# A two-block transformer kernel: the latents' compressed rows move from VectorE to ScalarE, VectorE's row work in 11 pieces

## The reference

```
c_kv, k_rope, k_g, v_g = split(kvc)          # 256, 32, 128, 128 columns
kv    = rms_norm(c_kv, g_ckv) @ w_ukv
k_gqa = apply_rope(rms_norm(k_g per head, g_kn_gqa))
c_q, q_g = split(qc)                         # 384, 512 columns
q_mla = rms_norm(c_q, g_cq) @ w_uq
q_gqa = apply_rope(rms_norm(q_g per head, g_qn_gqa))
y = sigmoid(gates) * branches
```

## Time and profile before

| | us |
|---|---|
| median of three executions | 2631.74 |
| the profiled execution | 2632.22 |
| its span | 2630.4 |
| TensorE matmuls busy | 2502.9 (95%) |
| VectorE busy | 1617.4 (61%) |
| ScalarE busy | 1325.9 (50%) |
| GpSimd busy | 585.1 (22%) |

### The profile page before, as it was taken

How to read it: one execution, slowest core, us unless ns; L and a number is a source line. 1 busy time by engine, 2 the same in 40 slices (tenths; PEclk the granted TensorE clock), 3 DMA queues, 4 the chain that set the end, 5 groups by cost and what they waited for, 6 DMA issues and landing times. The chain is left out here.

```text
span 2630.4 us, 46361 instructions
## 1 busy us (share of the span) xinstructions
PE 2502.9 (95%) x17358; PEld 2210.2 (84%) x17358; DVE 1617.4 (61%) x2415; ACT 1325.9 (50%) x2127; POOL 585.1 (22%) x429
## 2 busy tenths in 40 slices
PE   6999999999899998899999999997999999989998
PEld 5876899888599988875899899886998799758986
DVE  3655777566467756764777465545665654556545
ACT  3444565443546645445476455444544554445544
POOL 1110333221022321110233233020231232112311
PEclk9999999999999999999999999998999999989999
DMA  8565555555245655465556566562465466524663
GB/s 280 179 223 198 164 168 183 180 163 184 89 129 169 192 164 161 137 207 173 166 170 191 170 210 197 170 201 87 129 187 195 151 191 197 165 84 139 189 201 120
DMA packets 332946, 450.55 MB, mean 171 GB/s; under 512 B 28192, under 2 KB 207392, under 8 KB 332768
## 3 DMA queue, kind: packets, MB, share of 16 engines
q1 hardware_dynamic: 332400, 446.58, 53.9%
q0 software_dynamic: 368, 1.57, 0.2%
HBM read 446.99 MB, written 1.05 MB: 170 GB/s over the span
## 5 line engine op out<-in xcount | busy, mean ns | idle before, releaser
L740 DVE TENSOR_TENSOR wlo<-raw,whi 128x1024 fp32r<-128x1024 f32 (+4 forms) x631 | 806.3, 1290 | 660.1 <-ACT whi L734 655.5
L734 ACT CAST whi<-raw 128x1024 fp32r<-128x1024 f32 (+2 forms) x776 | 768.5, 1007 | 670.6 <-PE S L1037 236.8
L1053 PE MATMUL S<-hhi,whi 128*128 128x256 f32 x1952 | 546.9, 280 | 3.4 <-DVE wlo L740 1.8
L1053 PE MATMUL S<-hlo,whi 128*128 128x256 f32 x1952 | 544.7, 280 | 1.2 <-DVE hlo L1930 1.1
L1053 PE MATMUL S<-hhi,wlo 128*128 128x256 f32 x1952 | 544.6, 279 | 0.0
L740 POOL TENSOR_TENSOR wlo<-raw,whi 128x1024 fp32r<-128x1024 f32 (+3 forms) x145 | 338.4, 2334 | 712.2 <-ACT whi L734 711.3
L1053 PEld LDWEIGHTS S<-hhi,whi 128*128 128x128 f32 x1952 | 366.5, 188 | 5.2 <-issue 3.6
L1053 PEld LDWEIGHTS S<-hlo,whi 128*128 128x128 f32 x1952 | 366.3, 188 | 1.8 <-DVE hlo L1930 1.7
L1053 PEld LDWEIGHTS S<-hhi,wlo 128*128 128x128 f32 x1952 | 366.4, 188 | 0.0
L1053 PE MATMUL G<-hhi,whi 128*128 128x256 f32 x1088 | 305.6, 281 | 1.1 <-DVE wlo L740 0.7
L1053 PE MATMUL G<-hlo,whi 128*128 128x256 f32 x1088 | 302.4, 280 | 0.1
(11 more groups left out here) (368 smaller groups left out, 4456.2 us busy)
## 6 DMA issues: line engine op xcount, KB each, us to landing
raw<-in_ffn_wi SPq DMA_DIRECT2D x352, 256.0 KB, 3.6
raw<-in_w_up SPq DMA_DIRECT2D x264, 256.0 KB, 3.4
modw<-in_w_mod SPq DMA_DIRECT2D x192, 256.0 KB, 4.7
raw<-in_w_in SPq DMA_DIRECT2D x192, 256.0 KB, 3.0
raw<-in_ffn_wo SPq DMA_DIRECT2D x160, 256.0 KB, 3.6
raw<-in_w_down SPq DMA_DIRECT2D x120, 256.0 KB, 3.3
raw<-in_a_wqkv SPq DMA_DIRECT2D x72, 256.0 KB, 3.0
raw<-in_w_o SPq DMA_DIRECT2D x48, 256.0 KB, 3.4
```

What stands on the lines that cost most here:

```text
L734: act.copy(whi[:, n0 % SPLIT, z, w], raw[:, n0 % RAW, z, w]).then_inc(hi_done, 1)
L740: eng.tensor_tensor(wlo[:, n0 % SPLIT, z, w], raw[:, n0 % RAW, z, w], whi[:, n0 % SPLIT, z, w].bitcast(F32), ALU.subtract)\
L1053: mm = pe.matmul(out_[:, m * T:(m + 1) * T], w, x, start=first and c == 0 and m == 0 and z == 0, stop=last and c == kc - 1 and z == len(te ...
```

## The change

For the latents ("shared" stages, layers 0 and 1) ScalarE takes over the compressed rows. At the start of the first gate stage it computes the four mean squares (256 and 384 columns, two tiles) with an accumulating square, each waiting for the one before by `rows_squared`. Behind the casts of the second unit, ahead of that unit's sigmoids, it copies the grouped values and scales the compressed columns of both tiles, and signals `rows_scaled`. VectorE leaves these out, adds the epsilon to all twelve columns of `ms` (it waits for `rows_squared` first), and waits for `rows_scaled` ahead of the last key copy of each tile. Five of its 16 yields per stage fall away, so that `prep_rows` gives 11 pieces: the second piece holds the second tile's squares per head, its epsilon, the wait for the first tile's powers and the first tile's key scale and gain. All other stages emit what they did.

```
--- before.py
+++ after.py
@@ -513,6 +513,8 @@
         diag_done = sem("diag_done")
         rsum_done = sem("rsum_done")
         rsb_ready = sem("rsb_ready")
+        rows_squared = sem("rows_squared")
+        rows_scaled = sem("rows_scaled")
         old_turned = sem("old_turned")
         factor_diag = sem("factor_diag")
         order_done = sem("order_done")
@@ -671,6 +673,8 @@
 
 
             return sgained if source_of(st).kind == "pproj" else ybuf
+
+        shared = [st for st in STAGES if st.kind == "prep" and st.full and st.s == LAT]
 
         def tail(st):
 
@@ -1424,7 +1428,28 @@
                                 row_squares(early(st), t)
                     units(st, rows_in)
                 elif st.kind == "gates":
+                    prep = before(st, "prep")
+                    if prep in shared and st.part == 0:
+                        for t in range(NT):
+                            for z, (c0, n) in enumerate(((0, KV_RANK), (C_CQ, Q_RANK))):
+                                if t or z:
+                                    act.wait_ge(rows_squared, 4 * shared.index(prep) + 2 * t + z)
+                                act.activation(squared[:, 0:n], qkv1[:, t, c0:c0 + n], ACT.Square, scale=n ** -0.5,
+                                               accum_out=ms[:, t, z:z + 1]).then_inc(rows_squared, 1)
+
+                    def scaled_rows(prep):
+
+                        for t in range(NT):
+                            act.wait_ge(rs_ready, prep.rq + t + 1)
+                            act.copy(vg[:, prep.s * NT + t], qkv1[:, t, C_VG:C_CQ].rearrange("p (k d) -> p k d", d=DH))
+                            for z, (c0, n) in enumerate(((0, KV_RANK), (C_CQ, Q_RANK))):
+                                c = slice(c0, c0 + n)
+                                ins = act.activation(qkv1[:, t, c], qkv1[:, t, c], ACT.Copy, scale=rs[:, t, z:z + 1])
+                            ins.then_inc(rows_scaled, 1)
+
                     def sigmoids(k, j, i):
+                        if k == 1 and prep in shared and st.part == 0:
+                            scaled_rows(prep)
                         for b in range(2):
                             bank(st, b, k)
                             act.activation(gT[:, at((st.part * st.units + k) * 4 + 2 * b, 2), :], acc(st, j, b).rearrange("p (m t) -> p m t", m=2),
@@ -1708,9 +1733,10 @@
                 wait_units(dve, bank_free, st.u)
                 for t in range(NT):
                     ckv = q1[:, t, 0:KV_RANK]
-                    link(dve.tensor_tensor_reduce(scratch[:, 0:KV_RANK], ckv, ckv, 1.0 / KV_RANK, EPS, ALU.mult, ALU.add,
-                                                  ms[:, t, 0:1]))
-                    if st.full:
+                    if st not in shared:
+                        link(dve.tensor_tensor_reduce(scratch[:, 0:KV_RANK], ckv, ckv, 1.0 / KV_RANK, EPS, ALU.mult, ALU.add,
+                                                      ms[:, t, 0:1]))
+                    if st.full and st not in shared:
                         cq = q1[:, t, C_CQ:C_QG]
                         link(dve.tensor_tensor_reduce(scratch[:, KV_RANK:KV_RANK + Q_RANK], cq, cq, 1.0 / Q_RANK, EPS,
                                                       ALU.mult, ALU.add, ms[:, t, 1:2]))
@@ -1719,16 +1745,24 @@
                     if st.full:
                         head_squares(q1[:, t, C_QG:C_F], GQA_H, DH, ms[:, t, 4:12], scratch)
                         w = 12
-                    yield
-                    dve.tensor_scalar(ms[:, t, 2:w], ms[:, t, 2:w], EPS, None, ALU.add).then_inc(ms_ready, 1)
-                    yield
+                    if st not in shared:
+                        yield
+                    first = 2
+                    if st in shared:
+                        first = 0
+                        dve.wait_ge(rows_squared, 4 * shared.index(st) + 2 * t + 2)
+                    dve.tensor_scalar(ms[:, t, first:w], ms[:, t, first:w], EPS, None, ALU.add).then_inc(ms_ready, 1)
+                    if not (t and st in shared):
+                        yield
                 for t in range(NT):
                     dve.wait_ge(rs_ready, st.rq + t + 1)
-                    link(dve.tensor_copy(vg[:, st.s * NT + t], q1[:, t, C_VG:C_CQ].rearrange("p (k d) -> p k d", d=DH)))
-                    link(dve.tensor_scalar(q1[:, t, 0:KV_RANK], q1[:, t, 0:KV_RANK], rs[:, t, 0:1], None, ALU.mult))
-                    if st.full:
+                    if st not in shared:
+                        link(dve.tensor_copy(vg[:, st.s * NT + t], q1[:, t, C_VG:C_CQ].rearrange("p (k d) -> p k d", d=DH)))
+                        link(dve.tensor_scalar(q1[:, t, 0:KV_RANK], q1[:, t, 0:KV_RANK], rs[:, t, 0:1], None, ALU.mult))
+                    if st.full and st not in shared:
                         link(dve.tensor_scalar(q1[:, t, C_CQ:C_QG], q1[:, t, C_CQ:C_QG], rs[:, t, 1:2], None, ALU.mult))
-                    yield
+                    if st not in shared:
+                        yield
                     groups = [(C_KG, GQA_KV, 2, "kg")] + ([(C_QG, GQA_H, 4, "qg")] if st.full else [])
                     for c0, h, m, gain in groups:
                         x3 = q1[:, t, c0:c0 + h * DH].rearrange("p (h d) -> p h d", h=h)
@@ -1743,6 +1777,8 @@
                     if not st.full:
                         rope_keys(st, t)
                     link(dve.tensor_copy(kdup1[:, t, :, 0], k3))
+                    if st in shared:
+                        dve.wait_ge(rows_scaled, NT * shared.index(st) + t + 1)
                     dve.tensor_copy(kdup1[:, t, :, 1], k3).then_inc(rows_ready, 1)
                     yield
```

## The result

| | median us (lowest to highest) | runs | profiled execution us | its span us | granted clock |
|---|---|---|---|---|---|
| before | 2631.84 (2623.59 to 2633.38) | 8 | 2632.22 | 2630.4 | 0.982 |
| after | 2615.80 (2613.22 to 2622.42) | 8 | 2620.34 | 2618.2 | 0.985 |

The medians differ by 16.0 us; the ratio is 0.9941 [0.9929, 0.9952], 0.59% faster, where 10.7 us or 0.4% were forecast. The times lie inside the range of 2613 to 2631; the forecast of 2621 is 5 us too slow.

What follows compares the result with a forecast made beforehand. TensorE, 95% busy, was held to lose time only to idle and low clock behind late row work; two stages' 48.33 us become 36.98, less up to 0.3 us each, 10.7 us gained: 2631.74 - 10.7 gives 2621 us, range 2613 to 2631.

Steps and rivals of the forecast that it cites:

- What bounds: Latents' gate stages: TensorE idles about 4.8 us for row work left behind the last split, by order, not amount.
- The start: Stage start: four squares on ScalarE take 2.6 us ahead of the cast; split 1 ends 553.0, needed at 555.7.
- The middle: Splits 2 to 6 each ready before TensorE needs them; thinnest cover 1.1 us, at split 3.
- two engines shutting each other out: VectorE's second-tile squares beside GpSimd's powers: full exclusion lands powers 2.1 us later, gain 2.0 us smaller.
- The new wait: Piece 6, first tile's last key copy: VectorE idles 0.9 us for ScalarE's scaled rows; TensorE does not notice.
- so I take its end as the same: Layer 1 meets the same ScalarE release at T0 + 21.1, so its rows end as in layer 0.
- The end of layer 0: Last key copy at 581.0, gate matmuls end at 581.17: the wait is gone by 0.2 us.
- The sum: Both stages behind the gates: 48.33 us become 36.98, 10.7 us gained after late rows, 9.5 of it bare idle.
- the template of 18.49 us: Layer 0's context stage, rows in time: 5.57 + 12.92 us behind the gates, taken for both changed stages.
- Rival 2: Behind the gates of both stages the clock comes back wholly: 13.5 us gained, 2618 us; chance 0.10.
- Rival 4: Split queued behind late key copies stalls TensorE 3.7 us at slot 10: slower, 2634 to 2636 us; chance 0.05.
- Rival 3: Time handed back later by a queue that was just in time: 0 to 3 us left, 2630; chance 0.10.

Runs made afterwards that it cites:

- e1: Kernel before with the two latents' stages' row work in 12 pieces instead of 16, VectorE doing all of it; 2621.39 us, ratio 0.9949.
- e2: Changed kernel with the 16 pieces of before, ScalarE still doing the compressed rows; 2631.18 us, ratio 0.9993.
- e6: Changed kernel in 12 pieces with only the squares on ScalarE, value copies and scalings back on VectorE; ratio 0.9939.
- e8: Changed kernel, 11 pieces, squares back on VectorE, value copies and scalings on ScalarE behind its 6th and 7th cast; ratio 0.9952.
- e4: Kernel before with 40 unused matmuls issued on TensorE ahead of the wait for the rows in both stages; 2630.82 us, ratio 0.9986.
- after2: Changed kernel run again without any edit, for a second trace and more times; ratio 0.9938.
- e5: Changed kernel with ScalarE's scaled rows behind its 6th and 7th cast instead of the 8th; 2618.64 us, ratio 0.9944.
- e3: Changed kernel with the change limited to layer 0's latents; 2623.76 us, ratio 0.9961.
- e7: Changed kernel with ScalarE's scaled rows of both tiles only behind its 10th cast instead of the 8th; 2632.13 us, ratio 0.9990.
- before2: Kernel before run again without any edit, for a second trace; ratio 0.9999.

## Why the prediction was right, and where not

- **What bounds: right.** Order and not amount: e1 keeps the amount of VectorE's work and reaches 0.9949, e2 keeps the old order and gains nothing. That was read from four pieces behind the last split.
- **The start.** The squares' price was right (2.25 against 2.6 us). That they cost TensorE nothing was right as well, but the prediction did not say that they give VectorE nothing (e6).
- **The middle.** No split was late. The wait for the powers (0.2 us) did not appear, so none of the 2.0 us was lost that the prediction had weighed for two engines shutting each other out. The powers took 3.18 us as before, and the squares beside them were not slower (0.69 us for 512 columns, with and without). What the 3.19 us of the earlier trace rows held is told at the end.
- **The new wait.** 1.28 us in layer 0 against 0.9, inside the band of 0.5 to 1.5. In layer 1 VectorE stood 2.83 us and TensorE waited 0.62 us for the rows. Still "so I take its end as the same" held, counted from the stage's first gate matmul: VectorE came to its key copy 1.9 us earlier in layer 1 (19.17 against 21.03 us), and so stood longer, the copy began at 22.00 us against 22.31, and the last copy ended at 33.45 against 33.76. What failed was the cover. The gate matmuls took 32.72 us in layer 1, not 34.00; under 34.00 the rows would have been 0.5 us early. With the scalings early they are 1.6 us ahead at 32.73 us too (e8).
- **The end of layer 0**: rows 0.16 us ahead of the gates, 0.2 forecast.
- **The sum: the step that failed.** The bare idle was right (2 x 4.76 us, now 0 and 0.62). The clock was mis-sized, by the template of 18.49 us from the context stage of layer 0: it leaves 1.8 us for the clock, and e4 measured 3.7 to 4.3. Behind gates without a wait the touched stages took 17.03 us in layer 0 of after and after2, but 18.36 and 18.33 in e5 and e8; the context stage shows the same two outcomes. It is not changed by any of these kernels, and from its first gate matmul to the next gates it took 50.96 or 50.97 us in after, after2, e2, e3, e7 and e8, and 52.36 to 52.59 us in before, before2, e1, e4, e5 and e6 (50.96 is 33.92 + 5.22 + 11.82). The template was the slow one of the two. Both executions of before had it, and both of after the fast one, so these traces do not say whether chance or the kernel picks.
- **What the gain is made of.** With 17.03 us for both stages the sum is 48.33 - 2 x 17.03 = 14.3 us; 1.3 us of faster gate matmuls in layer 1 are added and its pause of 0.78 us taken off, 14.8 us, and after2's two stretches show 8.04 + 6.67 = 14.7. The context stage's 1.5 us between its two outcomes (52.41 to 50.96) makes it 16.2. Whether the change has a part in this 1.5 and in the 1.3 us is open: both traces of before lack them and both of after have them, but no experiment shows a way from one to the other. Rival 2 (13.5 us, "the clock comes back wholly") was nearest; I gave it 0.10 for the template's sake, when layer 1's own 11.82 us at 1.00, behind a pause of 4.9 us, already spoke for it. Even its 17.39 us for a stretch were more than the 17.03 measured.
- **How much of it was luck.** A gain of over 0.5% had a chance of 0.25 in the prediction. The range of 18 us held, but it reached to within 0.7 us of the median before and would have held nearly any small gain; it says little for the mechanism, and the waits say more.
- **The profiled execution of after** shows only 12.2 us less in span, after2's 16.4. Of the 4.3 us between these two, 1.3 lie in layer 1's stretch (clock 0.88 and 0.92 against 1.00 and 1.00) and 2.7 in the context's work from 169 to 238 us (0.95 against 1.00), long before the first touched stage. The ratios of the medians decide: 0.59 and 0.62%, 15.5 to 16.3 us.
- **Rival 4** was priced at 0.5 us worse per stage plus the clock, with a stall of 3.7 us at slot 10. e7 had 3.8 and 4.1 us and a ratio of 0.9990: the mechanism and the stall are right, the end 5 to 7 us better than the 2634 to 2636 forecast: against the stretches of before it was 0.2 us shorter in layer 0 and 1.1 us longer in layer 1.
- **Rival 3** (handed back later) is out: in after the two stretches are 8.04 + 5.37 = 13.4 us shorter and the span 12.2, in after2 14.7 and 16.4; nothing of size is given back behind them.

Left open: how much the scalings on ScalarE are worth beyond e1. e1, e5, e6, e8 and the change lie between 0.9938 and 0.9952 with intervals of 0.0012 to 0.0015 to each side; by the traces it is the 1.4 and 0.3 us of e1's waits. None of them beats the change by more than can be told apart.

## What to carry to other kernels

Where a helper engine's work is cut into pieces between its main tasks, count the pieces behind the last task first: moving work to another engine did nothing here until the cuts were changed, and the cuts alone did nearly all. An operation that is moved to another engine ahead of something that the first engine needs can delay it by as much as it spares. A stretch taken as the template for "what it will be without the wait" should have its clock counted with both ends: here a second execution of before gave the same 52.4 us again, and only the traces of other kernels showed the 50.96.

## What the runs showed of the hardware

**The clock behind a pause differs between executions of one kernel.** In layer 1 of before TensorE stood idle for 4.76 us and then had 0.69 and 1.00 over the transposes and the matmuls behind them (6.53 and 11.82 us). The second execution of the same kernel, behind 4.77 us, had these:

```profile
1108.78:1115.67 6.89, 5.40 (x23) 4.20 (x23) 3.99 (x6) 3.39 (x8) 2.14 (x2) 0.50 0.00 0
1115.67:1128.54 12.87, 12.87 (x63) 11.63 (x62) 6.42 (x11) 5.81 (x10) 1.01 (x1) 0.91 0.45 128
```

After and after2 differ in the same way behind 0.62 us of idle (5.63 and 12.78 us against 5.28 and 11.82). Nor does the length of the pause order the outcomes: behind 1.4 us the clock was 1.00 (e1), behind none 0.88 and 0.92 (e5, layer 0). Only the filled pause of e4 and the idle one of before are a pair that differs in nothing else. What decides between the outcomes was not found.

**GpSimd's powers take 0.9 us longer when a low-part subtraction has just begun on VectorE.** In layer 0 of before this subtraction began 0.17 us ahead of the powers, which took 3.19 us; in layer 1 VectorE stood still, and they took 2.27 us.

```profile
554.91 1.22 DVE L740 TENSOR_TENSOR wlo<-raw,whi 128x1024 fp32r<-128x1024 f32 x1
...
1074.45 2.27 POOL L2275 TENSOR_TENSOR rs<-ms,mhalf 128x12 f32<-128x12 f32 x1 [19.65 <-DVE ms L1723]
```

It is so in the latents' gate stages of all twelve traces: 3.17 to 3.25 us in the 28 cases with such a subtraction under way at the start, 2.27 to 2.33 us in the 20 without. The exclusion that the prediction weighed is seen in this one direction: GpSimd lost about the rest of VectorE's instruction, and VectorE's squares beside the powers lost nothing. The 3.2 us of the forecast had this loss in it already.

**Matmuls of 256 columns have two steady paces at a granted clock of 1.00.** The "up" matmuls of layer 0's latents, TensorE's windows of before:

```profile
830.00:840.00 10.00, 10.00 (x87) 1.00 0.57 176
840.00:850.00 10.00, 10.00 (x87) 1.00 0.64 197
```

and of e2's profiled execution:

```profile
830.00:840.00 10.00, 10.00 (x91) 1.00 0.51 160
840.00:850.00 10.00, 10.00 (x91) 1.00 0.72 215
```

87 against 91 matmuls in 10 us: by their starts one comes every 117.7 ns or every 113.3 ns, and e2's loop keeps its pace from its first slots to its end. Over both latents' "up" loops together, some 100 us each, e2's profiled execution took 8.9 us less than before's. It lies 10.5 us below its own median; that the other executions of e2 ran at the slower pace, as the other eleven traces did, is likely but not shown, since they were not traced. About the same pace took layer 1's gate matmuls from 34.00 to 32.72 us in after, after2, e6 and e8 and not in the others. There the two traces of before agree with each other, and the two of after, so the 1.3 us may belong to the kernel; the cause is open.
